# Three input projections of an even layer in exact split form, with the input tokens fetched a second time

## What is computed

```python
hp = rmsnorm(yp, norm_mix_g[l])
proj = h @ w_in
a_val, a_gate, z, xbc, dt_raw = jnp.split(proj, [...])
a_glu = a_val * jax.nn.sigmoid(a_gate)
a_conv, new_conf_state = causal_dwconv(a_glu, conf_state, conf_w, conf_b)   # width 31
a_out = jax.nn.silu(layernorm(a_conv, ln_g, ln_b))
xbc_c, new_xbc_state = causal_dwconv(xbc, ssd_conv_state, xbc_w, xbc_b)     # width 4
xbc_c = jax.nn.silu(xbc_c)
# ... the SSD scan over xs, b_in, c_out, dt; its output gated by silu(z) ...
out = jnp.concatenate([a_out, b_out], axis=-1) @ w_out
```

## Time and profile before

| | |
|---|---|
| median of 3 runs | 1749.54 us (1748.26 to 1749.71) |
| profiled execution: time / span | 1749.37 us / 1747.5 us |
| PE busy | 1707.0 us, 98% of the span |
| DVE / ACT / POOL busy | 1059.2 / 683.6 / 370.2 us |
| chain that ended last, by engine | PE 92%, DVE 4%, ACT 2% |
| granted PE clock, mean | 0.997 |

### The profile page before, as it was taken

The page is one execution under the profiler, slowest core; times in us unless marked ns, Lnnn a source line. Parts: engine busy times, 40 slices in busy tenths (PEclk is TensorE's granted clock), DMA queues, the critical chain, the costliest instruction groups (busy, mean ns, idle before and its releaser), DMA issues.

```text
span 1747.5 us, 27689 instructions
## 1 busy us (share of the span) xinstructions
PE 1707.0 (98%) x11360; PEld 1546.2 (88%) x11360; DVE 1059.2 (61%) x1717; ACT 683.6 (39%) x1219; POOL 370.2 (21%) x289
## 2 busy tenths in 40 slices
PE   7999998999999999999999999999999999999999
PEld 6566556897999999999989898679889999999999
DVE  3699867647677647465654325645566774655564
ACT  4111243334534525253542134533543453444352
POOL 3012100211104223132213133100110241414240
PEclk9999999999999999999999999999999999999999
DMA  8222330142304140403133123402421313212212
GB/s 261 103 79 97 98 118 11 49 193 97 109 25 140 39 136 23 134 26 127 36 129 73 74 73 138 170 27 76 191 73 43 127 40 112 70 61 94 86 67 91
DMA packets 39674, 162.30 MB, mean 93 GB/s; under 512 B 9384, under 2 KB 10280, under 8 KB 25600
## 3 DMA queue, kind: packets, MB, share of 16 engines
q1 hardware_dynamic: 32240, 124.59, 21.0%
q0 software_dynamic: 7312, 35.98, 5.7%
HBM read 149.87 MB, written 10.42 MB: 92 GB/s over the span
## 4 chain that ended last, share of the span: by engine, by line
PE 92%; DVE 4%; ACT 2%; issue 1%; DMA 0%; POOL 0%; SPq 0%; DVEq 0%; ACTq 0%
PE G L940 68%; PE S L940 12%; PE Q L940 11%; ACT work L1726 1%; PE Q L1640 1%; DVE rstd L2337 0%; ACT rstd L1726 0%; DVE ev_low L2586 0%; DMA ring<-in_w_mk 0%; DVE stats L2616 0%; DVE resid L2868 0%; ACT h_split L1726 0%; DVE stats L2985 0%; PE Q L1347 0%; DVE work L2629 0%
## 5 line engine op out<-in xcount | busy, mean ns | idle before, releaser
L940 PE MATMUL G<-ffn_rows,w_split 128*128 128x320 f32 x2160 | 329.8, 309 | 0.0
L940 PEld LDWEIGHTS G<-ffn_rows,w_split 128*128 128x128 f32 x2160 | 320.1, 188 | 0.0
L1726 ACT ACTIVATE w_split<-ring 128x512 fp32r<-128x512 f32 (+2 forms) x224 | 159.1, 711 | 316.7 <-PE G L940 208.3
L940 PE MATMUL G<-front,ring 128*128 128x128 f32 (+2 forms) x832 | 222.7, 429 | 10.9 <-DMA ring<-in_w_mk 9.1
L940 PEld LDWEIGHTS G<-front,ring 128*128 128x128 f32 x832 | 132.6, 193 | 99.7 <-issue 95.7
L856 POOL TENSOR_TENSOR mkT<-ring 128x512 f32<-128x512 f32 x72 | 97.7, 1362 | 564.5 <-DMA ring<-in_w_up 381.5
L940 PE MATMUL G<-h_split,w_split 128*128 128x320 f32 x1344 | 200.9, 310 | 1.2 <-DVE w_split L2352 0.9
L940 PEld LDWEIGHTS G<-h_split,w_split 128*128 128x128 f32 x1344 | 197.5, 188 | 1.9 <-issue 1.3
L940 PE MATMUL G<-g_split,w_split 128*128 128x320 f32 x1056 | 163.7, 310 | 0.1
L940 PEld LDWEIGHTS G<-g_split,w_split 128*128 128x128 f32 x1056 | 156.6, 188 | 1.6 <-DVE w_split L2841 1.3
L2708 DVE TENSOR_TENSOR w_split<-ring,w_split 128x512 fp32r<-128x512 f32 (+1 forms) x124 | 105.9, 856 | 60.3 <-ACT w_split L1726 59.1
(11 more groups left out here) (351 smaller groups left out, 2801.1 us busy)
## 6 DMA issues: line engine op xcount, KB each, us to landing
ring<-in_w_up SPq DMA_DIRECT2D x44, 1024.0 KB, 4.7
ring<-in_w_down SPq DMA_DIRECT2D x48, 256.0 KB, 2.6
ring<-in_w_down SPq DMA_DIRECT2D x32, 320.0 KB, 2.9
front<-in_mem_k POOLq DMA_DIRECT2D x8, 1024.0 KB, 6.8
front<-in_mem_v POOLq DMA_DIRECT2D x8, 1024.0 KB, 11.1
ring<-in_w_mk SPq DMA_DIRECT2D x4, 1024.0 KB, 6.2
ring<-in_w_mv SPq DMA_DIRECT2D x4, 1024.0 KB, 11.0
ring<-in_w_glu SPq DMA_DIRECT2D x4, 1024.0 KB, 8.9
```

The costliest lines, as they stand in the source:

```text
L940: return nc.tensor.matmul(out, lhsT, rhs, start=start, stop=stop, **kw)
L1726: return nc.scalar.activation(*a, **k)
```

## The change

The 8 `glu`, 8 `xbc` and 4 `z` tiles take the split form (`mix_product`, `mix_terms`). In code:

```diff
@@ buffers
+        with nc.sbuf_tensor("mix_high", [P, KD, T], F32R) as mix_hi:
+            pass
         x = sb("resid", [P, KD, T])
+        mix_w = overlay("mix_weights", MIX_AT, 2, KD, P)
@@ GpSimd
+            def mix_low(q):
+                pool.wait_ge(mix_high, q + 1)
+                src, hi, lo = mix_piece(q)
+                nc.gpsimd.tensor_tensor(lo, src, hi.bitcast(F32), ALU.subtract).then_inc(mix_split, 1)
             memory_keys(0)
+            mix_low(0)
+            mix_low(1)
             for j in range(4):
+                if j < 3:
+                    mix_low(2 * j + 2)
+                    mix_low(2 * j + 3)
                 read_wait(pool, TILE0["glu"] + 2 * j + 1)
                 store(...)
             memory_keys(1)
+            mix_low(8)
+            mix_low(9)
             for j in range(KD):
-                if j == 6:
-                    (waits, then the load of h0T)
+                mix_low(10 + j)
                 read_wait(pool, xbc_tile(j))
                 store(...)
+            for q in range(18, 20):
+                mix_low(q)
+            (waits, then the load of h0T)
+            tile_wait(pool, z_tile(3))
+            pool.dma_start(x[:, :, :], dram["x"][:, :, :]).then_inc(x_again, 16)
@@ TensorE
-            projections("glu", 8, KD, rows(h), norm="mix0")
-            narrow(TILE0["dtp"], "wdt", h)
+            for q in range(2):
+                begin(mix_tile(q))
+                pe.wait_ge(mix_split, q + 1)
+                mix_terms(q, (0, 1), False)
+            for q in range(2):
+                mix_terms(q, (2,), True)
+            for q in range(2, 8):
+                mix_product(q)
+            narrow(TILE0["dtp"], "wdt", (mix_hi.bitcast(F32), ev_lo.bitcast(F32)))
...
-            projections("xbc", 8, KD, rows(h), after=lambda n: n == 5 and conv_stat(3))
+            for j in range(KD):
+                mix_product(8 + j)
+                if j == 5:
+                    conv_stat(3)
@@ ScalarE
+            def mix_weights(q):
+                c = mix_chunk(q)
+                act.wait_ge(chunk_in[c % RING], 16 * (c // RING + 1))
+                if q >= 2:
+                    tile_wait(act, mix_tile(q - 2))
+                else:
+                    act.wait_ge(mem_key_eps, 4)
+                src, hi, _ = mix_piece(q)
+                A(hi, src, ACT.Copy).then_inc(mix_high, 1)
+            def mix_high_row(k):
+                act.wait_ge(applied, APPLIED["mix0"] - KD + 1 + k)
+                A(mix_hi[:, k, :], h[:, k, :], ACT.Copy).then_inc(mix_rows_hi, 1)
@@ VectorE
+            for k in range(KD):
+                dve.wait_ge(mix_rows_hi, k + 1)
+                v.tensor_tensor(mix_low_row(k), h[:, k, :], mix_hi[:, k, :].bitcast(F32), ALU.subtract)\
+                    .then_inc(mix_rows, 1)
-                conv_taps(32 if j < 3 else 44)
+                conv_taps(24 if j < 3 else 44)
@@ VectorE, before evout's residual addition
+            dve.wait_ge(x_again, 16)
```

More of the change, by code:

```diff
@@ L474, in evout_piece, with mix_tile, mix_chunk, mix_piece @@
             return src, ev_w[:, i % 2], lo
+        MIX = [("glu", i) for i in range(8)] + [("xbc", i) for i in range(8)] + [("z", i) for i in range(4)]
+        def mix_tile(q):
+            name, i = MIX[q]
+            return z_tile(i) if name == "z" else TILE0[name] + i
+        def mix_chunk(q):
+            name, i = MIX[q]
+            return CHUNK[name] + i // 2
+        def mix_piece(q):
+            at = mix_chunk(q) % RING
+            src, lo = (w[:, at, :].rearrange("p (k n) -> p k n", k=KD)[:, :, q % 2 * P:(q % 2 + 1) * P]
+                       for w in (ring, ring_r))
+            return src, mix_w[:, q % 2], lo
+        def mix_low_row(k):
+            return ev_lo[:, k, :]
         def odout_piece(i):
@@ L1041, in narrow @@
                 pe.wait_ge(par_in if wname == "wdt" else wf_ready, 16 if wname == "wdt" else 1)
-                for k in range(KD):
-                    q, o = k % 4, PAR[wname][0] + k * NH
-                    rows, w = slice(32 * q, 32 * q + 32), par[:, o:o + 32]
-                    mm(out[rows, 0:512], w, rows_of[:, k, 0:512], k < 4, k >= 4, tile_position=(0, 32 * q))
-                    m = mm(out[rows, 512:T], w, rows_of[:, k, 512:T], k < 4, k >= 4, tile_position=(0, 32 * q))
+                for part, rows_part in enumerate(rows_of):
+                    for k in range(KD):
+                        q, o = k % 4, PAR[wname][0] + k * NH
+                        rows, w = slice(32 * q, 32 * q + 32), par[:, o:o + 32]
+                        first, last = part == 0 and k < 4, part == len(rows_of) - 1 and k >= 4
+                        mm(out[rows, 0:512], w, rows_part[:, k, 0:512], first, last, tile_position=(0, 32 * q))
+                        m = mm(out[rows, 512:T], w, rows_part[:, k, 512:T], first, last, tile_position=(0, 32 * q))
                 m.then_inc(tile_done, 1)
@@ L1120, in _ @@
             memory_values(1)
-            projections("xbc", 8, KD, rows(h), after=lambda n: n == 5 and conv_stat(3))
-            s = chunk(CHUNK["z"])
-            for n in range(2):
-                project(z_tile(n), s, n % 2 * P, KD, rows(h))
+            for j in range(KD):
+                mix_product(8 + j)
+                if j == 5:
+                    conv_stat(3)
+            for j in range(2):
+                mix_product(16 + j)
             nready[0] += 4
@@ L1138, in _ @@
                 .then_inc(tile_done, 1)
-            s = chunk(CHUNK["z"] + 1)
-            for n in range(2, 4):
-                project(z_tile(n), s, n % 2 * P, KD, rows(h), halfway=h_free if n == 3 else None)
+            for j in range(2, 4):
+                mix_product(16 + j, h_free if j == 3 else None)
             RUN, CSK = NCH - 1, 64 + NH
@@ L1563, in _ @@
                 if c == NCH - 1:
-                    narrow(TILE0["fp"], "wf", x)
+                    narrow(TILE0["fp"], "wf", (x,))
                 frame_major_split(fv_tile(c), c)
@@ L1854, in memory @@
                 for m2 in range(2):
+                    mix_weights(8 + m2)
                     memory_values(l, m2)
@@ L1877, in _ @@
                     read_wait(act, t0 + 2 * (j - 2) + 1)
-                evacuate(tmp[:, j % 2, :], t0 + 2 * j, ACT.Sigmoid)
+                evacuate(tmp[:, j % 2, :], t0 + 2 * j, ACT.Sigmoid, out=GF)
+                if j < 3:
+                    mix_weights(2 * j + 2)
+                    mix_weights(2 * j + 3)
             act.wait_ge(par_in, 16)
@@ L1888, in xbc_rows @@
                 a, b = padded(xbcp, j, XW - 1, XPROMPT, XREQ, XW - 1)
-                A(a, G[n % 2][:, 0:SEQ], ACT.Copy)
-                A(b, runs(G[n % 2][:, SEQ:T]), ACT.Copy).then_inc(read[n % 2], 1)
+                A(a, GF[n % 2][:, 0:SEQ], ACT.Copy)
+                A(b, runs(GF[n % 2][:, SEQ:T]), ACT.Copy).then_inc(read[n % 2], 1)
+                mix_weights(10 + j)
             def xbc_silu(j):
@@ L1897, in z_gate @@
             def z_gate(j):
-                evacuate(zs[:, j, :], z_tile(j), ACT.Silu)
+                evacuate(zs[:, j, :], z_tile(j), ACT.Silu, out=GF)
+                if j < 2:
+                    mix_weights(18 + j)
             act.wait_ge(dt_abs, 1)
```

46 lines of the change are left out of this document (39 added, 7 removed).

## The result

The changed kernel takes 1786.22 us (median of 4 runs, 1784.25 to 1788.38), against 1748.9 us before on the same chip: 1.0213 times the time, with a 95% interval of 1.0197 to 1.0229. It is slower, as forecast, but by 37 us and not by 24.7. That is 1.2 us beyond the upper end of the range. The profiled execution took 1784.25 us, with a span of 1782.5 us and a mean granted clock of 0.981 (0.997 before).

The account below looks back on a forecast made before the run. PE bounds the whole launch, but DVE's chain to z1 has only 2.7 us of slack; with POOL's subtractions holding DVE, the scan starts 22.6 us later, plus 2.1 slow start: 1749.37 + 24.7 = 1774.1 us, range 1760 to 1785.

Parts of the forecast that it names:

- The bound and the chain: Ahead of z1: the chain taps, sum, squares, xbc_rows(7) has only 2.7 us of slack against PE.
- PE's tiles: 20 split tiles at 7.15 instead of 8.68 us save 31 us; narrow costs 2.40 again; 28 us on PE alone.
- The first pair: At the first two tiles: tile 1 ends at 66.0, so DVE's chain of taps starts 1.0 us late.
- The price p: DVE's loss to one mix_low on POOL: 2.3 us taken, with bounds of 0 and 2.9.
- POOL's subtractions, the costly part: Fourteen subtractions before the first conv_sum ends each hold DVE 2.3 us; that sum ends at 223.3 instead of 194.95.
- Rival C: POOL waits for DVE at mix_low(17), 18 and 19; scan up to 8 us later, 1782 us; 13 in 100.
- The clock: PE's slow start after standing idle, taken once, for z1 behind 11 us of idle: 2.1 us.
- The sum: Total: scan 22.6 us later plus 2.1 for the slow start, 24.7 us on 1749.37, giving 1774.1 us.
- Rivals A and B: A: POOL never holds DVE, 1746.8 us, 8 in 100; B: PE's 28 us all arrive, 1722.6, 3 in 100.

Follow-up runs that it names:

- before_with_subtractions: The kernel before, plus fourteen same-size POOL subtractions at the places of mix_low 2 to 15, which no other engine waits for: 1767.41 us, 1.0103.

## Why the prediction was right in sign and short in size

**The bound and the chain: right, where POOL is served.** With the memsets, 14 us of PE work moved into PE's wait gains nothing (1769.65 against 1769.99): DVE's chain to `z1` is what counts, and the plain gain of PE's tiles does not come through. In the changed kernel itself the way to `z1` ran through PE's two waits for POOL and ACT's copy of `xbc` tile 5.

**PE's tiles: right.** A split tile takes 6.98 us (7.15 forecast), `narrow` 2.40 a second time. PE's busy time fell by 19.7 us and not by 28; the 5.9 us of slow restarts are most of the difference.

**The first pair: right.** The first GLU product came at 66.58 (66.0) and tile 2 at 68.44 (67.9). But the other products still waited for PE (1.65, 0.80, 1.55 us), which the forecast had ruled out: PE itself had waited 2.00, 0.85 and 1.68 us for POOL, which was kept out here too (the subtraction at 77.43 took 5.92 us).

**The price p: right.** 2.14 us measured for 2.3. In the two kernels where POOL is served at once DVE's sum ends at 224.7 and 219.6, around the forecast 223.3, and the scan starts at 285.05 and 280.53, around the forecast 284.

**The step that failed: that POOL gets its turn.** The prediction's sum lets all fourteen subtractions take place beside the taps, each at once, with DVE held for it ("POOL's subtractions, the costly part"), and puts PE's wait of 31 us at `conv_stat(3)`. In the changed kernel two of them were kept out and took 57.91 us together, PE waited 15.79 and 20.26 us for them at `xbc` tiles 1 and 2, and nothing at `conv_stat(3)`. A memset every 8 taps takes this away and brings the forecast picture and 16.2 of the 37.3 us. Rival C had the mechanism, from a row of 3.46 us instead of 0.72, and its 1782 us was the nearest of the rivals' numbers. That nearness is luck in part, since it limited the wait to the few taps of that row and looked for it ahead of `z1`. The length of the wait is what is left of the run that POOL meets, and in the memory and `xbc` stretch a run has 60 taps. Ahead of `z1` there is no such run, since the `xbc` taps come in runs of 6, and `mix_low(17)` took 2.44 us.

The rule of the Trainium skill that I set beside that row ("SBUF — State Buffer", section "Who interferes with whom": whoever issues first has the shared ports for its instruction, the other blocks) gave a wait of one tap at most. The measurement decides against that reading: 54 and 60 taps went by. What the section does have right is that taps with both inputs in SBUF collide with POOL, and that DVE stands still for POOL's length (2.14 of 2.4 us). The one-input taps of this kernel are held as well: 2.94 us instead of 0.8 for the pair at 175.50.

**The clock: right for `z1`, two restarts missed.** For `z1` 2.1 us were forecast and 1.9 measured. The other two restarts, 4.0 us, came with the two waits that the forecast did not have; keeping PE at work there brought `z1` 2.35 us forward.

**The sum.** Forecast for `z1` 257.2 and measured 268.92, 11.7 us later; from there to the scan 26.3 us against 24.9 and the 2.1 for the clock. So the miss lies wholly ahead of `z1`.

**Rivals A and B** are out: p is not 0, and the plain gain of 28 us was reached by no kernel; the best got 2.3 us of it, and one without the subtraction 7.7.

Open is what keeps POOL out, and when exactly. "Until the run ends" fits the long waits, but it is no strict rule. In the kernel before, two key products got in under way in a run of 14 two-input taps, the one at 132.20 that took 8.59 us. They came 3.7 and 5.9 us into it, and took 1.14 and 0.75 us, where one alone takes 0.72. POOL's timeline of the kernel before:

```profile
135.89 1.14 POOL L779 TENSOR_TENSOR mkT<-mkT,rstd 128x256 f32<-128x256 f32 x1 [2.10 <-ACT rstd L1726]
138.08 0.75 POOL L779 TENSOR_TENSOR mkT<-mkT,rstd 128x256 f32<-128x256 f32 x1
```

Two more POOL instructions stood at the beginning of that same run (132.18 and 133.00), which may matter. Against that, in `before_with_subtractions` one that came 1.8 us into a run (175.84) waited for all the rest of it. What the runs do show is that a gap of 0.12 us between taps or a memset lets POOL in, that it also gets in behind the first tap of a fresh run (the subtraction at 83.88 took 2.81 us, 0.2 us behind the start of 24 taps), and that otherwise it waited for up to 60 taps. How often a break is needed (every 16 or 30 taps) was not tried.

## What to carry to other kernels

A GpSimd instruction that reads SBUF is not slowed by a long back-to-back run of two-input VectorE instructions, it can be shut out until the run ends (60 taps here); so before giving GpSimd work that TensorE waits for, count the length of VectorE's runs at that place, and look in the trace for a short GpSimd instruction that is drawn far too long. If the work must stay, a break every few instructions is nearly free (31 memsets of 0.06 us), though VectorE still pays 2.14 us for each subtraction; if it can go to VectorE, it costs a little over half of what it costs as interference (1.22 against 2.14 us), but needs places where its input is there. And where PE is full on the page, its gain can be no larger than the slack of the chain beside it: shorten that chain first.

## What the hardware showed

- 60 two-input taps back to back (27.82 us) stretched a 2.4 us subtraction of GpSimd to 27.9 and then another to 30.0 us, without slowing down at all.
- In a run of 14 such taps (8.59 us) GpSimd's 0.72 us products got in under way, with 1.14 and 0.75 us.
- Where GpSimd does get in, VectorE stands still for 2.14 of its 2.4 us; a pair of one-input taps is held as well (2.94 us instead of 0.8).
- One memset of a single element (0.06 us) every 8 taps brought nearly every subtraction back to 2.4 to 2.9 us (one took 5.17) and the kernel 16 us.
- A wait on the instruction directly ahead costs DVE 0.12 us a tap, and lets GpSimd in as well.
- After idle stretches of 8.8 to 20 us TensorE's granted clock was 0.50 for the first 2.8 to 5.5 us; a tile of 7.0 us took 8.4 to 9.6.
